# Eleven more weight remainders of a streaming encoder step move from VectorE to GpSimd, in quarters

## The reference

```python
xn = rmsnorm(x, attn_pre_norm)
h = xn @ w_in
(g_q, g_k, g_v, g_low, g_r, a_q, a_k, a_v, i_q, i_k, i_w, gate_logits) = jnp.split(h, splits, axis=-1)
log_a = jax.nn.log_sigmoid((g_low @ w_gla_gate_up + b_gla_gate).astype(jnp.float32)) / GLA_GATE_TAU
gla_o, gla_s = gla_recurrence(...)          # 4 heads, S_t = diag(a_t) S_{t-1} + k_t^T v_t, o_t = q_t S_t
gla_o = rmsnorm(gla_o, gla_head_norm) * jax.nn.silu(g_r)
dsa_o = dsa_mixer(...)                      # sparse attention over keys chosen by an indexer's top-k
gate_a, gate_b = jnp.split(jax.nn.sigmoid(gate_logits), 2, axis=-1)
mixed = (gate_a * (gla_o @ w_branch_gla) + gate_b * (dsa_o @ w_branch_dsa)) @ w_out
x = x + rmsnorm(mixed, attn_post_norm)
f, conv_new = conv_ffn(rmsnorm(x, ffn_pre_norm), conv_prev, w_up, conv_w, conv_b, w_down)
x = x + rmsnorm(f, ffn_post_norm)
```

## Time and profile before

| | before |
|---|---|
| median of 3 runs | 982.27 us (981.74 to 982.34) |
| profiled execution, whole | 983.36 us |
| its span, first to last instruction | 981.6 us |
| PE busy | 960.3 us (98%) |
| VectorE (DVE) busy | 615.1 us (63%) |
| ScalarE (ACT) busy | 476.7 us (49%) |
| GpSimd (POOL) busy | 175.5 us (18%) |
| mean granted clock of TensorE | 0.994 of full speed |

### The profile page before, as it was taken

One profiled execution on the slowest core, in us unless ns is written; L12 is line 12 of the kernel. 1 busy time (PEld: TensorE's weight loads), 2 busy tenths in 40 slices (PEclk: granted clock), 3 DMA queues, 4 the chain that ended last, 5 costly groups with the idle time before them and its releaser, 6 DMA issues.

```text
span 981.6 us, 17131 instructions
## 1 busy us (share of the span) xinstructions
PE 960.3 (98%) x6556; PEld 909.9 (93%) x6556; DVE 615.1 (63%) x996; ACT 476.7 (49%) x800; POOL 175.5 (18%) x301
## 2 busy tenths in 40 slices
PE   7998999999999999999999999999999999999997
PEld 5998999999999999999998899999999999788885
DVE  5367778845435348934446587788888889722214
ACT  6356346777322255522124457566666667522112
POOL 3104242222111211001001144211111111200000
PEclk9999999999999999999999999999999999999999
DMA  6722112111376557776446451334444334312323
GB/s 167 168 80 84 47 44 87 43 44 44 95 254 207 175 189 242 259 284 207 143 134 225 139 172 49 102 120 128 121 144 131 118 118 139 123 53 86 133 71 118
DMA packets 121835, 129.75 MB, mean 132 GB/s; under 512 B 14867, under 2 KB 103811, under 8 KB 119474
## 3 DMA queue, kind: packets, MB, share of 16 engines
q1 hardware_dynamic: 115330, 105.97, 34.8%
q0 software_dynamic: 6448, 22.99, 6.6%
HBM read 105.84 MB, written 23.11 MB: 131 GB/s over the span
## 4 chain that ended last, share of the span: by engine, by line
PE 90%; ACT 4%; DVE 3%; issue 1%; POOL 1%; DMA 0%; SPq 0%; ACTq 0%; DVEq 0%; POOLq 0%
PE ps L2068 10%; PE ps L2070 10%; PE ps L2069 10%; PE ps L2077 7%; PE ps L2408 7%; PE ps L2078 7%; PE ps L2079 7%; PE ps L2410 7%; PE ps L2409 7%; PE ps L2248 2%; PE ps L2087 2%; PE ps L2088 2%; PE ps L2383 1%; PE ps L2385 1%; PE ps L2384 1%
## 5 line engine op out<-in xcount | busy, mean ns | idle before, releaser
L2068 PE MATMUL ps<-xs,whi 128*128 128x288 f32 x608 | 184.5, 303 | 0.0
L2070 PE MATMUL ps<-xs,wlo 128*128 128x288 f32 x608 | 180.2, 296 | 0.0
L2069 PE MATMUL ps<-xs,whi 128*128 128x288 f32 x608 | 180.1, 296 | 0.0
L1524 DVE TENSOR_TENSOR wlo<-raw,whi 128x2048 fp32r<-128x2048 f32 (+2 forms) x36 | 79.2, 2201 | 107.3 <-ACT whi L956 107.3
L956 ACT ACTIVATE whi<-raw 128x2048 fp32r<-128x2048 f32 (+2 forms) x47 | 86.1, 1831 | 97.7 <-PE ps L2079 74.9
L2068 PEld LDWEIGHTS ps<-xs,whi 128*128 128x128 f32 x608 | 115.3, 190 | 0.7
L2069 PEld LDWEIGHTS ps<-xs,whi 128*128 128x128 f32 x608 | 115.2, 189 | 0.4
L2070 PEld LDWEIGHTS ps<-xs,wlo 128*128 128x128 f32 x608 | 115.0, 189 | 0.0
L2077 PE MATMUL ps<-whi,xs 128*128 128x256 f32 (+2 forms) x232 | 76.6, 330 | 1.5 <-ACT v_tok L1024 1.5
L2078 PE MATMUL ps<-whi,xs 128*128 128x256 f32 (+2 forms) x232 | 74.8, 322 | 0.0
L2079 PE MATMUL ps<-wlo,xs 128*128 128x256 f32 (+2 forms) x232 | 74.7, 322 | 0.0
(11 more groups left out here) (364 smaller groups left out, 2600.7 us busy)
## 6 DMA issues: line engine op xcount, KB each, us to landing
raw<-in_w_in SPq DMA_DIRECT2D x21, 1024.0 KB, 5.7
raw<-in_w_down SPq DMA_DIRECT2D x10, 1024.0 KB, 5.0
saved<-in_w_up SPq DMA_DIRECT2D x36, 256.0 KB, 4.4
sums_scratch<-saved SPq DMA_DIRECT2D x9, 1024.0 KB, 4.9
raw<-sums_scratch SPq DMA_DIRECT2D x9, 1024.0 KB, 4.9
qraw<-in_w_up SPq DMA_DIRECT2D x27, 256.0 KB, 2.9
raw<-in_w_up SPq DMA_DIRECT2D x13, 512.0 KB, 4.1
raw<-in_w_up SPq DMA_DIRECT2D x26, 256.0 KB, 4.5
```

The source lines that it names most:

```text
L1524: nc.vector.tensor_tensor(wlo[:, p % 2, 0:n], raw[:, p % 2, 0:n], whi[:, p % 2, 0:n].bitcast(F32), ALU.subtract).then_inc(lo_ready, 1)
L2068: pe.matmul(out, wh[:, k, c0:c0 + P], xh[:, k, t], start=(k == 0), stop=False)
L2069: pe.matmul(out, wh[:, k, c0:c0 + P], xl[:, k, t], start=False, stop=False)
L2070: ins = pe.matmul(out, wl[:, k, c0:c0 + P], xh[:, k, t], start=False, stop=(k == kn - 1))
```

## The change

`POOL_SPLITS` is the list of panels whose remainder GpSimd writes. It held panels 5 to 13. It now also holds 14 to 24, so all remainders of the input projection from panel 5 on are GpSimd's.

```diff
-POOL_SPLITS = [s.panel + 1 for s in SLOTS[8:AT_GLA - 12] if s.opens]
+POOL_SPLITS = [s.panel + 1 for s in SLOTS[8:] if s.opens and s.panel + 1 < BRANCH0]
```

## The result

| | before | after |
|---|---|---|
| median | 982.0 us (981.43 to 982.34, 4 runs) | 997.56 us (997.12 to 999.33, 4 runs) |
| ratio | | 1.0162 (95%: 1.0145 to 1.0180) |
| profiled execution, whole | 983.36 us | 999.33 us |
| its span | 981.6 us | 997.1 us |
| PE busy | 960.3 us | 965.5 us |

The change makes the kernel 15.6 us slower; 15.0 us were forecast. The measured median lies 0.3 us from the forecast of 997.3 us. The profiled execution of the change is the slowest of its four. Of what it takes more than the profiled one before (16.0 us), 15.5 us lie in the span and 0.5 us outside of it: 1.8 us outside before, 2.2 us now.

The account below looks back on a forecast made before the run. PE was taken to bound the kernel, busy throughout 225 to 450 us. Two waits (10.8 us) plus clock falls (4.2 us) made 15.0 us, added to the 982.27 us median: 997.3 us, range 993 to 1000.5 us.

Parts of the forecast that it names:

- PE has nothing to win between 225 and 450 us: In the eleven panels' stretch PE is always busy, so taking 25.2 us of work off VectorE was costed at nothing.
- Two waits of 5.4 us: Slots 64 and 68: q_tile queues behind the split on GpSimd, so PE's step b waits twice, 10.8 us in all.
- The clock: Behind each wait PE's clock falls to half: 2.1 us per wait, 4.2 us in all, bounds 0 to 3.1 each.
- The mask in slot 60: Slot 60: VectorE's mask copy, later behind GpSimd's split, ends at 288.2 us against PE's use at 289.05; no wait.
- Rival 2: VectorE and GpSimd block each other, output gates' norm sums come late: 0.4 to 4.2 us, 998 to 1001.5 us; chance 0.10.
- What was costed at nothing: Panel remainders 2.7 us later, later raw-buffer loads, and stores and silu loads at most 5 us late: no cost.
- The price of a split: GpSimd's four 128x512 subtractions per panel: 5.02 us from the trace; the skill's smaller price would give 9.7 us of waits.
- Busy times: In the changed profile VectorE should be busy 25 us less and GpSimd 55 us more.

Follow-up runs that it names:

- the nine panels alone: Kernel before, with nine of the eleven panels moved to GpSimd and 17 and 18 left on VectorE: 981.05 us, ratio 1.0004.
- the two versions with 800 units: Kernel before with VectorE's top-k room per slot cut from 1600 to 800: 978.39 us; also with eleven panels on GpSimd, q_tile ahead of the split: 978.73 us.
- the moved q_tile: The change, but GpSimd builds q_tile before the split in slots 64 and 68: 982.60 us, 1.0014 against the kernel before.
- panels 17 and 18 alone: Kernel before, with only panels 17 and 18 (slots 64 and 68) also moved to GpSimd: 994.12 us, ratio 1.0132.
- the doubled split: The change, with every quarter of panels 17 and 18 computed twice: 1006.91 us, 1.0254 against the kernel before.
- the repeated change: The change run again unaltered, on one chip beside the kernel before: 997.00 us, ratio 1.0145.
- the filled kernel: The change, with 40 useless PE matmuls before step b of the second and fourth token tile: 993.41 us, 1.0109 against the kernel before.
- the first filled kernel: The change, with 37 useless PE matmuls before step b of the second and fourth token tile: 993.67 us, 1.0132 against the kernel before.

## Why the prediction was right

- **PE has nothing to win between 225 and 450 us.** Shown by the nine panels alone (1.0004) and by the two versions with 800 units, which differ in eleven panels and not in their spans.
- **Two waits of 5.4 us.** Measured 5.4 and 5.4. The split took 4.94 us instead of 5.02, and the hand-overs 0.1 us each. That the place alone makes them is shown by the moved q_tile (they vanish), by panels 17 and 18 alone (they stay) and by the doubled split (they grow one for one). This is the mechanism of the forecast, and it came as described.
- **The clock.** Taken as 2.1 us per wait, 4.2 in all, a value between two falls of the trace before. The profiled execution had 1.75 + 3.0 = 4.75 us, the repeated change 4.5 us by its rows, and the filled kernel gives 3.6 us by the medians. The bounds held (0 to 3.1 us per wait). Equal waits of 5.4 us cost differently, because the clock fell 2.1 us into the first (305.04 against 302.94) and 4.7 us into the second (342.58 against 337.85), and came back 6.8 us after each fall. Work at half clock lost 49% of its time (1.73 of 3.52 us, 3.00 of 6.16 us) where 46% was taken. That the sum of two such terms came within 0.6 us of 4.2 is in part luck.
- **The 0.3 us between forecast and median** are luck. The profile has 10.8 us of waits, 4.75 us of clock and 0.5 us outside the span, of which the last was not in the forecast at all. The medians of the kernel before alone go from 980.3 to 982.1 us over the chips. The 0.5 us also show in the moved q_tile and in both filled kernels (2.1 to 2.2 us outside the span against 1.7 to 1.8), and not with the split done twice (1.7 us), though all eleven panels are on GpSimd there too; what makes them stays open.
- **The mask in slot 60.** Worked out to end at 288.2 us; it ended at 287.54 + 0.74 = 288.28 us, and PE did not wait.
- **Rival 2, VectorE and GpSimd block one another.** The mechanism came as described: two-input products of VectorE took up to 1.88 us instead of 0.76, and splits 6.07 us instead of 5.02. The rule of the Trainium skill (SBUF — State Buffer, section Who interferes with whom: a VectorE instruction with two SBUF inputs contends with a GpSimd instruction that reads SBUF, and the lock on the shared ports is exclusive) agrees with these rows. The rival's price was too high. VectorE did not wait for a whole split: each product beside it took 0.2 to 1.1 us longer, two or three of four per split, and the sum of squares came 0.5 us before PE, where the rival's bound was 0.1 us behind. PE waited at no norm matmul. (The 0.4 us that the rival took for three such places should be 0.3 by its own 0.1 us each.)
- **What was costed at nothing and wasn't always.** The step said that a copy waits for PE's slots and not for its load. For slots 64 and 68 it held. For panel 24 it is wrong, as the trace before could have shown (421.96 us above): the copy waits for its load, and PE waited 0.7 and 0.8 us for the remainder in two of the seven profiles with eleven panels on GpSimd. The silu loads behind the split were costed at nothing because ACT needs a staging buffer only two units later. That says nothing of VectorE, which reads their data: it waited 0.63 us for one in the row above, at no cost to PE.
- **The price of a split.** The Trainium skill (GPSIMD Engine Reference, section 3.1) gives 4497 ns for one addition of 2048 elements. By that, as an estimate, each wait would have been 0.5 us shorter; four quarters took 4.94 us, so the trace's figure was the right one.
- **Busy times.** GpSimd's 55 us came (91.13 - 36.06), VectorE's 25 us came only as 15, for the blocking above.

## What to carry to other kernels

Before giving an idle engine more work, look in its program at what will stand behind the new instruction: its idle share (18% here) says nothing of whether a short helper, on which the busiest engine waits, now queues behind a long one that waits for a third engine. If the helper can run first, put it first; here that turned a loss of 1.6% into 0.1%. Moving work off an engine on which nobody waits brought nothing here, with 20.6 us of it gone.

## What the runs showed of the hardware

A wait of PE cost more than itself: behind two waits of 5.4 us the clock's fall cost 3.6 us more by the medians, 4.5 to 4.75 us by the rows, and useless matmuls in their place won that back. GpSimd took its program in order: q_tile, ready to run since PE's previous tile, started only when the split in front of it was done (307.26 us), and the split only when ACT's copy was (302.37 us).

Most of the scatter between executions of the kernel before goes with this clock: on one chip its spans go from 976.7 us at a mean clock of 1.00 to 981.1 to 982.0 us at 0.994, for the same instructions. A median of few runs can thus hide or invent 2 to 3 us, as it did between the first filled kernel and the one with two panels. Spans of the same mean clock scatter less, by 0.9 us at 0.994 and 1.7 us at 0.996 on that chip, where all 23 scatter by 5.3 us.
